# A routed sum in four row tiles: the combination of expert outputs with half of its zeros left out

## The reference

```python
scores = jax.nn.sigmoid(xf @ w_router)          # [256, 64]
# the best 4 of 8 groups, then the best 6 experts of a token
gate = gate / gate.sum(-1, keepdims=True) * ROUTED_SCALE
def expert_block(xs):
    tok, g, e = xs
    xb = x_pad[tok]
    hb = jax.nn.silu(xb @ w_exp_gate[e]) * (xb @ w_exp_up[e])
    return (hb @ w_exp_down[e]) * g[:, None]
routed = jax.ops.segment_sum(yb.reshape(n_rows, D), row_tok, num_segments=T + 1)[:T]
shared = (jax.nn.silu(xf @ w_sh_gate) * (xf @ w_sh_up)) @ w_sh_down
```

## Time and profile before

| | us |
|---|---|
| median of 3 runs (lowest, highest) | 1089.35 (1084.38, 1091.15) |
| the profiled execution | 1085.52 |
| its span in the trace | 1083.8 |
| TensorE busy, share | 1035.7, 96% |
| VectorE, ScalarE, GpSimd busy | 566.9, 397.6, 380.5 |
| HBM read | 318.72 MB, 295 GB/s over the span |

### The profile page before, as it was taken

The page is one execution under the profiler, slowest core; times in us unless marked ns, Lnnn a source line. Parts: engine busy times, 40 slices in busy tenths (PEclk is TensorE's granted clock), DMA queues, the critical chain, the costliest instruction groups (busy, mean ns, idle before and its releaser), DMA issues. The chain is left out here.

```text
span 1083.8 us, 12961 instructions
## 1 busy us (share of the span) xinstructions
PE 1035.7 (96%) x5024; PEld 689.5 (64%) x5024; DVE 566.9 (52%) x1023; ACT 397.6 (37%) x681; POOL 380.5 (35%) x309
## 2 busy tenths in 40 slices
PE   8999998999999899999999999999999989999995
PEld 7888886888788786788877444444444444543442
DVE  5899678766976786756666222222322222211243
ACT  5645765365434453657344112121211121111214
POOL 1499999679970298099100000000000000000000
PEclk9999999899999899999999999999999999999998
DMA  9766666466764667545379799999999999999992
GB/s 324 259 210 231 208 206 214 167 238 216 264 231 156 193 205 248 166 137 175 117 225 413 268 413 416 415 417 416 416 415 416 417 416 415 416 417 417 416 413 111
DMA packets 92461, 320.63 MB, mean 296 GB/s; under 512 B 8784, under 2 KB 11888, under 8 KB 75760
## 3 DMA queue, kind: packets, MB, share of 16 engines
q1 hardware_dynamic: 84448, 290.90, 69.9%
q0 software_dynamic: 7664, 28.37, 7.9%
q10 hardware_dynamic: 288, 0.52, 0.1%
HBM read 318.72 MB, written 1.05 MB: 295 GB/s over the span
## 5 line engine op out<-in xcount | busy, mean ns | idle before, releaser
L879 PE MATMUL ps<-hl,L 128*128 128x512 f32 (+1 forms) x1216 | 386.7, 400 | 6.5 <-issue 3.5
L879 PEld LDWEIGHTS ps<-hl,L 128*128 128x128 f32 x1216 | 229.1, 192 | 58.4 <-issue 10.9
L1783 DVE TENSOR_TENSOR rlo<-ring,hl 128x1024 fp32r<-128x1024 f32 (+1 forms) x154 | 215.5, 1420 | 86.3 <-ACT hl L1355 85.8
L879 PE MATMUL ps<-slots_all,xe 128*64 128x512 f32 (+1 forms) x1088 | 235.2, 574 | 8.9 <-DMA slots_all<-in_w_exp_up 8.0
L879 PE MATMUL ps<-rlo,L 128*128 128x512 f32 (+1 forms) x608 | 239.6, 394 | 0.0
L1355 ACT ACTIVATE hl<-ring 128x1024 fp32r<-128x1024 f32 (+1 forms) x154 | 159.2, 1054 | 151.7 <-PE ps L879 97.4
L868 POOL CAST two<-ident 64x128 fp32r<-64x128 f32 x64 | 18.9, 296 | 484.1 <-PE ps L879 482.6
L821 POOL TENSOR_SCALAR mring<-mring,st 128x512 f32<-128x512 f32 x84 | 172.0, 2048 | 1.6
L879 PEld LDWEIGHTS ps<-slots_all,xe 128*64 128x64 f32 x1088 | 81.1, 137 | 140.6 <-issue 135.1
L879 PEld LDWEIGHTS ps<-rlo,L 128*128 128x128 f32 x608 | 116.5, 192 | 24.5
L823 POOL TENSOR_TENSOR macc<-macc,mring 128x512 f32<-128x512 f32 x84 | 122.3, 1456 | 7.0
(11 more groups left out here) (233 smaller groups left out, 936.3 us busy)
## 6 DMA issues: line engine op xcount, KB each, us to landing
slots_all<-in_w_exp_gate SPq DMA_DIRECT2D x64, 1024.0 KB, 22.6
slots_all<-in_w_exp_up SPq DMA_DIRECT2D x64, 1024.0 KB, 21.4
slots_all<-in_w_exp_down SPq DMA_DIRECT2D x62, 1024.0 KB, 22.0
ring<-in_w_in SPq DMA_DIRECT2D x48, 1024.0 KB, 5.3
mring<-in_w_mod POOLq DMA_DIRECT2D x48, 512.0 KB, 4.3
ring<-in_w_out SPq DMA_DIRECT2D x8, 1024.0 KB, 5.0
ring<-in_w_ple_gate SPq DMA_DIRECT2D x4, 1024.0 KB, 5.6
ring<-in_w_branch_a SPq DMA_DIRECT2D x4, 1024.0 KB, 6.3
```

The source lines that it names most:

```text
L879: return e.matmul(o, l, r, start=start, stop=stop)
L1783: return e.tensor_tensor(o, a, b, op)
```

## The change

For pairs 0 to 27 the combination is made of 16 products of 32 rows in place of 8 of 128. Row group g (rows 32g to 32g + 31) is one tile of the array; it holds tokens of half g % 2 alone, so it is multiplied with these tokens' selectors only, and the half of the old products that had only zeros in the selector falls away. In one part the four groups write four different banks; in the other part the groups of one token half change feature halves. Groups g and g + 2 add to the same bank, and so part 1 waits on `comb` for the end of part 0. Between the parts stands `turn_p`. Pairs 28 to 31 keep the old form.

```diff
--- before.py
+++ after.py
@@ -1267,6 +1267,17 @@
                                  i < NG)
                 x.then_inc(comb, 1)
 
+            def combine_rows(i, part):
+                wait_read(("p", i), ("d", i, 0), ("d", i, 1))
+                if 2 * i + part:
+                    w.wait_ge(comb, 2 * i + part)
+                for q in range(2):
+                    for g in range(4):
+                        h, c, rows = g % 2, (g // 2 + part) % 2, slice(32 * g, 32 * g + 32)
+                        x = onto(4 + 2 * h + c, ppt[rows, i % 4, tok(h)], yy[rows, q, half(c)], i == NG - 1 and part == 1 and q == 1,
+                                 True)
+                x.then_inc(comb, 1)
+
             def combine_last(i):
                 wait_read(("p", i), ("d", i, 0))
                 for m in range(2):
@@ -1327,9 +1338,13 @@
                 turn_h(j - 1)
                 gate_up(j)
                 down(j - 1)
+                if 2 <= j < NG + 2:
+                    combine_rows(j - 2, 0)
                 if j + 1 < NP:
                     turn_p(j + 1)
-                if j >= 2:
+                if 2 <= j < NG + 2:
+                    combine_rows(j - 2, 1)
+                elif j >= 2:
                     combine_both(j - 2)
                 if j % 4 == 3 and j + 1 < NP:
                     gather(j // 4 + 1)
```

## The result

| | before | after |
|---|---|---|
| median of 20 runs (lowest, highest) | 1087.07 (1083.34, 1091.15) | 1090.57 (1089.01, 1095.76) |
| the profiled execution, its span | 1085.52, 1083.8 | 1090.47, 1088.6 |
| TensorE, share of the span | 96% | 95% |

The ratio after to before is 1.0039, with an interval of 1.0027 to 1.0051: slower by 2.9 to 5.5 us, at most about half of the 10.9 us bound. The time of 1090.57 lies 0.4 us from the forecast of 1090.2, but part of that is luck of the base. The forecast was +0.8 us on a median of three runs, 1089.35; twenty runs of the same kernel give 1087.07, and the change cost 3.5 us by the medians (4.2 by the ratio, which isn't that of the medians), not 0.8. Three executions of later kernels, one each of gfin_late, old_last3 and all_rows, took 2573, 4095 and 2586 us and aren't counted in their ratios.

The account below looks back on a forecast made before the run. Transfers at 416 GB/s were taken as the bound, hiding TensorE's 14 us gain; only +0.8 us for a clock fall was added to the 1089.35 us median, giving 1090.2 us, range 1083 to 1097.

Parts of the forecast that it names:

- Bound by the transfers: Expert stage: weight transfers need 15.12 us a pair, TensorE 14.1, so TensorE's gain does not reach the end.
- the 16.3 of the text: Pairs 2 to 31: TensorE's slack against the transfers, 424.5 us between starts less 408.2 needed.
- The rival that TensorE ends last: Expert stage: TensorE sets the end after all, so 8 to 20 us are gained, 1069 to 1081; chance 0.05.
- Row tiles side by side: Combination: four row tiles run together, 1.1 to 1.5 us a pair against 1.83; hidden by transfers, chance 0.56.
- one by one: Combination: row-tile products run in sequence, 16 x 0.229 = 3.66 us, a total of +40 to +51 us; chance 0.12.
- the estimate of 1.2 us: Combination: 16 x 0.229 / 3.07 from the skill's speedup; with tile switches a gain of 0 to 0.4 us a pair.
- the second sum: Combination: weight loads one behind the other, 2.1 to 2.5 us a pair, a loss of 0.3 to 0.7; chance 0.27.
- Moved: they serve the next pair, whose gate product is read a round later: Each round: the selectors' turn and VectorE's comparison and gate sums come some 0.6 us later; no cost was given.
- a gain of 0.5 us a pair: Combination of pairs 0 to 27: taken from 0.3 to 0.7 us; 14 us leave TensorE in all.
- The clock term: Pair 30's wait for up weights: 3.5 to 4.5 us, then a clock fall costing 1.7; half taken, +0.8 us.
- the likelier case: Behind pair 30's wait: the clock's fall, costing 1.7 us, becomes more likely than not.
- Pair 30's weights land as before: Pair 30's up weights land at 1038.2 us as before, since the transfers had no hole for an earlier slot.

Follow-up runs that it names:

- gfin_late: The kernel after, with GpSimd's 0.52 MB load of the last norm's gain waiting for pair 30's gate/up group; ratio to before 1.0004.
- old_last3: The kernel after, with the old combination form for pairs 25 to 27 as well; ratio to before 1.0009.
- all_rows: The kernel before with row tiles for pairs 0 to 30, selectors' product ahead of both parts, later gain load, four unused products ahead of pair 30; ratio 0.9994.
- no_comb: The kernel before without the combination products of pairs 0 to 26, whose outputs are missing from the sum; ratio 1.0003.
- pad: The kernel before with four unused products ahead of each gate/up group of rounds 2 to 29; ratio 1.0299, 32.5 us slower.
- turn_first: The kernel after with the selectors' product ahead of both parts of the combination; ratio to before 1.0025.
- hold: The kernel after with six unused products ahead of pair 30's gate/up group, in TensorE's last wait; ratio to before 1.0003.
- tile_order: The kernel after with loops swapped, so the two products of one row tile stand next to each other; ratio to before 1.0028.
- before_hold: The kernel before with four unused products ahead of pair 30's gate/up group, in TensorE's last wait; ratio 0.9993.
- tail_rows: The kernel before with row tiles for pairs 28 to 30 alone; ratio 0.9984.
- tail_hold: The kernel before with row tiles for pairs 28 to 30 alone and four unused products in TensorE's last wait; ratio 0.9988.
- tail_gfin: The kernel before with row tiles for pairs 28 to 30 alone and the last norm's gain loaded after pair 30's gate/up group; ratio 0.9987.

## Why the prediction was right, and where it was not

**Bound by the transfers: right, and shown from both sides.** Taking 49 us from TensorE gave nothing (no_comb), adding 48.4 gave 32.5 (pad), which puts the slack at 15.9 us against the 16.3 of the text. The rival that TensorE ends last needed a gain; no_comb has none.

**Row tiles side by side: right, with its price, though its terms are off.** Both parts take 1.35 us, in the range of 1.1 to 1.5, and one by one (3.66) is out. But the text had a round of four products at 0.229 us and the rest in changes of tile shape. In the trace the four products of a round start within 0.02 us of each other, and the next round or the next instruction follows 0.33 to 0.34 us later in both rounds of a part (681.58, 681.92, 682.25), so it is the round that is dearer; of the changes only the 0.09 us at the selectors' product shows. Against 3.66 the speedup is 2.7; the Trainium skill, TensorE: Matmul & The Clock Gate, Measured speedup vs the span model, has 3.07 for four row tiles at this size, and the estimate of 1.2 us worked out from it is near the 1.35 us measured with the switches. The same page of the Trainium skill, LDWEIGHTS, has a 32 x 128 load take as long as one of the whole array. That does not lead to the second sum here: eight such loads fit in 0.30 us.

**"Moved: they serve the next pair, whose gate product is read a round later": wrong.** This step put no price on the selectors' turn coming 0.6 us later. What it had as cover was the time until the sums are read; what counts is the bank they are made from, which the next gate/up group needs at once. The 21 waits of 7.8 us in the weight loads, and their going away in turn_first, show it. Of a gain of 0.5 us a pair 0.07 is left; the total is 4.6 us, not 14. It did no harm to the forecast, since neither reaches the end. The starts of gate/up are 12.86 us apart where the text asked for 12.4, the first wait comes before 852 us as asked, and the waits sum to 13.3 us where some 20 were due.

**The clock term: right in kind, half its size.** The text had a last wait of 3.5 to 4.5 us and 0.8 us, half of 1.7. The wait was 4.98, of which 1.36 is the later landing, which the text didn't have; the 3.6 that are left are as forecast. The 1.7 came whole; hold takes it back. It was the likelier case by the text's own words, and the predicted time should have been that of the likelier case, with 1.7 in it.

**"Pair 30's weights land as before": wrong by 1.4 us.** This was argued from a full transfer rate. The rate stayed, but a full rate doesn't fix when a given load ends. The text had only the weights in this stream; the loads of the engines' own instructions, which use the same DMA engines, it left out, and they are what moved.

Each load of weights comes in 16 parts and has landed with the last of them. Up to pair 30's first gate load the landings of before and after keep the same steps behind pair 27's. Its first up load then takes 25.5 us from issue to landing in after and 24.2 in before. In the trace's events fifteen of its parts land by 41.5 us behind pair 27's landing in after, where before had all sixteen; the last part lands at 42.85, and it stays some 1.3 us behind in every load from there on. While it was awaited, a 16 KB packet of the instruction queue (q8) was served, from 40.25 to 41.33 us. Here are that load in before and in after (KB, us from issue to landing), and the instruction queue in the 1.3 us of after around the packet (packets, MB, share):

```profile
slots_all<-in_w_exp_up SPq DMA_DIRECT2D x1, 1024.0 KB, 24.2
...
slots_all<-in_w_exp_up SPq DMA_DIRECT2D x1, 1024.0 KB, 25.5
...
q8 instruction: 1, 0.02, 5.2%
```

The other DMA engines go on with later loads meanwhile, so that SyncE's queue moves 19.3 MB between the two landings, 18.8 in before, and the rate shows nothing. The kernels fall into three groups, all times in us behind pair 27's landing:

| kernels | last instruction packet ahead of pair 30's landing starts at | last part behind the fifteenth |
|---|---|---|
| after, hold, turn_first, tile_order, gfin_late, all_rows | 39.3 to 41.6 | 1.32 to 1.48 |
| before, before_hold, tail_rows, tail_hold, tail_gfin | 33.9 to 34.3 | 0.03 to 0.13 |
| no_comb, old_last3 | 21.0, 21.2 | 0.05, 0.13 |

Where the packet moves, the late part moves with it: in hold it is served at 41.48 us and the next load is the first to be late; in old_last3 it comes at 52.97, behind pair 30's landing, and then one part of a load of pair 31 is late (55.27, the others by 54.12). The new form brings 448 more matmul and weight-load records on TensorE, and the page counts 43 instruction packets, 41 in before and 40 in no_comb. So the change did delay the landing, by more instructions and not by less work, but which load a packet hits is chance of its place: those of 34 us delay nothing at pair 30. That packet and late part share a DMA engine is inferred from their times, since the trace doesn't name the engine, and no run changed the instruction loads alone.

An earlier request is not what does it. SyncE issues pair 31's up weights 36.6 us behind pair 27's landing in after and 36.5 in before. These two issues take 5.68 us in after and 4.33 in before, but the packet is served during them.

**The sum.** Of the measured +3.5 us (2.9 to 5.5) the traces place 1.4 in the landing and 1.6 in the tail's clock. The forecast had 0.8 of them, and a base that was 2.3 us high.

## What to carry to other kernels

Where a load that lands last holds the end, making the engine that waits for it faster is worth nothing at best, and here it cost 3 us: a longer wait at which the clock falls, and more instructions, whose own loads pass through the same DMA engines and once hit the load that was waited for. Compare landings load by load, since a steady transfer rate hides one late part. Before an instruction is moved, ask of every bank it writes when the next writer needs it, not only when its result is read. A step that is only faster should be put where nothing waits behind it, here the last three combinations, and the wait kept filled; even then 1 us of 1087 is hard to tell from none.

## What the runs showed of the hardware

- Behind TensorE's last wait in after the granted clock was 0.66 over 1040 to 1045 us, a mean between the levels of 2.4 and 1.2 GHz, and the 29 records took 8.32 us, not 6.62. Waits of 2.98 us (old_last3), 3.00 (before) and 3.44 (no_comb) were not followed by such a fall; waits of 3.11 (tail_rows), 3.27 (before, pair 19), 3.70 (gfin_late), 4.98 (after), 5.01 (turn_first) and 5.04 (tile_order) were. In no_comb earlier waits of 2.99 to 3.02 us went either way: four were followed by 7.95 to 8.32 us for the 29 records, three by 6.62. Their length alone doesn't decide it.
- Sixteen float32r products on four row tiles of 32 took 1.35 us in two parts and 1.48 in one sequence with a wait between them, against 1.83 for eight on the whole array. Two products in a row on one tile cost no more than four tiles in turn (0.68 against 0.67 us a part).
- A whole-array product took 0.43 us to the next start with row tiles behind it (after, and turn_first with column tiles ahead of it), 0.34 with whole-array products behind it (before); going from column tiles to row tiles behind the down group cost nothing that shows (3.53 us, as before, where no wait precedes).
- A 16 KB packet of instructions, 1.1 us long, was followed by one part of sixteen of a 1 MiB load 1.3 us late while the rate stayed at 416 GB/s, and that part stayed late in the loads behind it (after, hold, old_last3).
- 0.52 MB on another queue delayed the landing of a load on a full set of DMA engines by 1.27 us, the time of its bytes at 416 GB/s, in the old form and in the new.
